# Sparse attention in one Trainium2 core: index scores, key choice and key/value products moved between the input projection's products, heads in pairs, 128 keys for the first 128 queries, token mixing in groups

## The reference

```python
xn = _rmsnorm(h, mix_norm_g[l]) * (1.0 + sc1) + sh1
proj = xn @ w_in[l]
q_a, kv_lat, q_i, k_i, w_i, p_shift, gate_a, gate_r = _split(proj, IN_SPLITS)
q = _rmsnorm(q_a by head, q_norm_g);  kv = _rmsnorm(kv_lat, kv_norm_g) @ w_kv_up
k_lin, v_lin = split(kv);  k = _rmsnorm(k_lin by head, k_norm_g)
o_attn = _dsa_attention(q, k, v, q_i, k_i, w_i)      # 8 heads of 64, 8 index heads of 32
o_rwkv = _rwkv7_time_mix(p_shift, mu, ...)
merged = sigmoid(gate_a) * (o_attn @ w_branch_attn) + sigmoid(gate_r) * (o_rwkv @ w_branch_rwkv)

# _dsa_attention, for a block of 128 queries at positions t
dots = einsum('bthd,bsd->bths', q_i, k_i)
score = einsum('bths,bth->bts', relu(dots), w_i) * idx_scale
score = where(key_pos <= t, score, -inf);   sel = top_k(score, 64)
logits = q . k[sel] / 8 - slopes[h] * (t - sel)      # slopes 2^-(h+1); masked where sel > t
o = softmax(logits) @ v[sel]

# _rwkv7_time_mix begins with
mixed = p_shift + (prev - p_shift) * mu              # prev: the token before
```

## Time and profile before

| | before |
|---|---|
| median of 3 runs | 2263.12 us (2263.04 to 2264.96) |
| the profiled execution's own time | 2260.12 us |
| its span in the trace | 2258.5 us |
| PE busy | 2089.4 us (93%) |
| DVE, ACT, POOL busy | 703.7, 277.7, 105.9 us |
| granted clock of PE, mean | 0.952 |

### The profile page before, as it was taken

How to read it: one execution, slowest core, us unless ns; L and a number is a source line. 1 busy time by engine, 2 the same in 40 slices (tenths; PEclk the granted TensorE clock), 3 DMA queues, 4 the chain that set the end, 5 groups by cost and what they waited for, 6 DMA issues and landing times.

```text
span 2258.5 us, 23974 instructions
## 1 busy us (share of the span) xinstructions
PE 2089.4 (93%) x9838; PEld 1249.5 (55%) x9838; DVE 703.7 (31%) x1237; ACT 277.7 (12%) x567; POOL 105.9 (5%) x142
## 2 busy tenths in 40 slices
PE   6999989999999999989999998586699799999998
PEld 2444444444444464457888887355588544444444
DVE  2565244424422055272433122636401400000001
ACT  2000010000000021251000011231100210000000
POOL 0010000000000020000111002000000000000000
PEclk9999999999999999999999999558899799999999
DMA  9333264424221350016774340014020699999997
GB/s 397 139 102 105 110 260 147 137 95 151 74 89 51 136 219 0 0 38 267 279 254 168 134 168 15 0 61 175 2 77 38 275 394 427 429 429 428 428 429 309
DMA packets 48186, 419.92 MB, mean 186 GB/s; under 512 B 5376, under 2 KB 5392, under 8 KB 22896
## 3 DMA queue, kind: packets, MB, share of 16 engines
q1 hardware_dynamic: 28800, 344.73, 37.5%
q0 software_dynamic: 18880, 71.18, 9.0%
q10 hardware_dynamic: 432, 2.95, 0.4%
HBM read 417.79 MB, written 1.05 MB: 185 GB/s over the span
## 4 chain that ended last, share of the span: by engine, by line
PE 81%; DVE 9%; DMA 6%; ACT 2%; issue 1%; DVEq 0%; ACTq 0%; SPq 0%; POOLq 0%
PE PS L799 17%; PE PS L816 10%; PE PS L974 8%; PE PS L1106 7%; PE PS L828 5%; DMA ring<-w_moe 4%; PE PS L962 4%; PE PS L1165 4%; PE PS L1126 4%; PE PS L1362 3%; PE PS L1139 2%; DVE SC L1443 2%; PE PS L932 2%; PE PS L773 2%; PE PS L943 2%
## 5 line engine op out<-in xcount | busy, mean ns | idle before, releaser
L799 PE MATMUL PS<-A,ring 128*128 128x512 f32 (+1 forms) x1408 | 466.3, 492 | 9.2 <-ACT A L490 9.2
L799 PEld LDWEIGHTS PS<-A,ring 128*128 128x128 f32 x1408 | 269.8, 193 | 193.9 <-issue 173.3
L816 PE MATMUL PS<-A,ring 128*128 128x512 f32 (+1 forms) x704 | 228.5, 486 | 3.2 <-DVE A L1502 3.2
L974 PE MATMUL PS<-ring,A 128*64 128x512 f32 x1024 | 223.4, 593 | 3.1 <-DMA ring<-w_moe 2.3
L816 PEld LDWEIGHTS PS<-A,ring 128*128 128x128 f32 x704 | 133.3, 190 | 96.1 <-issue 87.1
L1106 PE MATMUL PS<-A,ring 128*128 128x512 f32 x384 | 167.9, 598 | 2.0 <-ACT A L490 2.0
L974 PEld LDWEIGHTS PS<-ring,A 128*64 128x64 f32 x1024 | 73.9, 137 | 149.4 <-issue 142.7
L1443 DVE SCALAR_TENSOR_TENSOR SC<-A,CS,SC 128x512 f32<-128x512 f32 x208 | 143.7, 746 | 4.6 <-DMA A<-ada 2.2
L1106 PEld LDWEIGHTS PS<-A,ring 128*128 128x128 f32 x384 | 73.0, 192 | 91.4 <-issue 89.7
L828 PE MATMUL PS<-A,ring 128*128 128x256 f32 (+1 forms) x384 | 113.7, 458 | 9.2 <-DMA ring<-w_cout 6.8
L1502 DVE TENSOR_TENSOR A<-A,PS 128x512 f32 (+1 forms) x44 | 24.4, 554 | 304.2 <-ACT A L499 304.2
(11 more groups left out here) (308 smaller groups left out, 1976.7 us busy)
## 6 DMA issues: line engine op xcount, KB each, us to landing
ring<-w_moe SPq DMA_DIRECT2D x96, 2048.0 KB, 17.5
ring<-w_fin SPq DMA_DIRECT2D x44, 1024.0 KB, 8.1
ring<-ada POOLq DMA_DIRECT2D x64, 512.0 KB, 3.7
A<-ada POOLq DMA_DIRECT2D x64, 512.0 KB, 3.8
ring<-w_fout SPq DMA_DIRECT2D x16, 1408.0 KB, 6.1
ring<-w_conv SPq DMA_DIRECT2D x8, 1536.0 KB, 12.6
ring<-w_qkv SPq DMA_DIRECT2D x6, 2048.0 KB, 16.3
ring<-w_win SPq DMA_DIRECT2D x6, 2048.0 KB, 11.3
```

What stands on the lines that cost most here:

```text
L799: mm = pe.matmul(PS[:, 2 * (s % 3) + half, 0:T], slot(stage, s, k * 256 + half * 128, k * 256 + half * 128 + 128), h_of(k, T), start=(k == ...
L816: mm = pe.matmul(PS[:, s, 0:T], slot(stage, s, k * 128, k * 128 + 128), HID[:, k * T:(k + 1) * T], start=(k == 0), stop=(k == KF - 1))
L974: mm = pe.matmul(PS[CAP * e:CAP * (e + 1), g, :], XG[:, k * P + e * CAP:k * P + (e + 1) * CAP], slot("moe", k // 2, w, w + 512), start=(k ...
```

## The change

Five things are done, all in the third block.

*Order of the projection.* Key and value products, their head norms and the index scores are written in between the projection's products. The latent's sum of squares comes after product 4 instead of 10, `w_i` after product 8 instead of 14, head 0's dots after product 9. Banks are given explicitly.

*First block with 128 keys.* `keys(t)` is 128 for the first block of queries and 256 for the second; dots, relu, scores, key choice, attention and mixing use it.

*Key choice.* `NEGM` is made at the start of the stretch. The two blocks' MAX and MATCH_REPLACE wait for each other by counts of the semaphore `top` instead of `link`. Rounds and number of keys stay the same.

*Heads in pairs.* `dsa_attention` has the form of `na_attention`: 8 pairs, two heads in rows 0 to 63 and 64 to 127, four score banks, four buffers for probabilities. The bias matmul is gone: POOL makes the slopes times distance for all 8 heads ahead (`BIAS1`), DVE adds `SEL` once for all heads, and one DVE instruction adds the bias and takes the row maximum.

*Mixing in groups.* POOL mixes five chunks at a time, as soon as these are copied, in three groups.

```diff
+        BIAS1 = X[:, 2048:4096].rearrange("p (h t) -> p h t", h=HEADS2)
+        BIAS0 = A[:, 14848:15872].rearrange("p (h t) -> p h t", h=HEADS2)
+        def keys(t):
+            return P * (t + 1)
...
+            pool.wait_ge(sem("dist_in"), 16)
+            for h in range(HEADS2):
+                pool.tensor_scalar(BIAS1[:, h, :], DIST[:, 1, :], -(2.0 ** -(h + 1)), None, ALU.mult).then_inc(
+                    sem("bias_made"), 1)
...
-            pool.wait_ge(sem("win_copied"), len(COPIES))
             pool.wait_ge(sem("lat_done"), 2)
-            pool.tensor_tensor(d3[:, :, 1:SEQ], p3[:, :, 0:SEQ - 1], p3[:, :, 1:SEQ], ALU.subtract).then_inc(sem("mixed"), 1)
-            pool.tensor_scalar(d3[:, :, 0:1], p3[:, :, 0:1], -1.0, None, ALU.mult).then_inc(sem("mixed"), 1)
...
+            for g in range(3):
+                a, b = 5 * g, 5 * g + 5
+                pool.wait_ge(sem("win_copied"), copies_to(9 + b - 1))
+                pool.tensor_tensor(d3[:, a:b, 1:SEQ], p3[:, a:b, 0:SEQ - 1], p3[:, a:b, 1:SEQ], ALU.subtract).then_inc(
+                    sem("mixed"), 1)
...
+                pool.tensor_tensor(p3[:, a:b, :], p3[:, a:b, :], d3[:, a:b, :], ALU.add).then_inc(sem("mixed"), 2)
...
+            def dots(h):
+                r = 32 * (h % 4)
+                if h == 0:
+                    pe.wait_ge(sem("lat_root"), 1)
+                    pe.wait_ge(sem("wi_done"), 1)
+                    copied(8)
+                if h >= 2:
+                    pe.wait_ge(sem("relu"), 2 * (h - 1))
+                for t in range(2):
+                    pe.matmul(PS[:, 6 + h % 2, t * 256:t * 256 + keys(t)], QI[r:r + 32, h // 4, t * P:(t + 1) * P],
+                              KI[r:r + 32, 0:keys(t)], start=True, stop=True, tile_position=(r, 0)).then_inc(sem("dots"), 1)
...
+            for j in range(4):
+                if j < 2:
+                    copied(8 + 2 * j)
+                else:
+                    pe.wait_ge(sem("hn_done"), 20 + j - 1)
+                key_product(j, 2 * (j % 2))
+                copied(9 + 2 * j if j < 2 else 10 + j)
+                win_product(12 + j, (2 * j + 1) % 4)
+                head_stat(20 + j, 4 + j % 2)
+                dots(3 + j)
+            pe.wait_ge(sem("hn_done"), 23)
+            value_product(0, 0)
+            copied(14)
+            win_product(16, 1)
+            dots(7)
+            pe.wait_ge(sem("hn_done"), 24)
+            value_product(1, 2)
+            copied(15)
+            win_product(17, 3)
...
+            copied(23)
+            pe.wait_ge(sem("relu"), 16)
+            dsa_attention()
...
-                    pe.matmul(PS[:, u % 2, 0:256], ident, BI[:, u % 2, :], start=False, stop=True).then_inc(
-                        sem(f"s_{t}"), 1)
...
+                    for h in range(2):
+                        r = 64 * h
+                        mm = pe.matmul(PS[:, 2 * (p % 2) + h, 0:keys(t)], QA[r:r + 64, hp, t * P:(t + 1) * P],
+                                       KA[r:r + 64, hp, 0:keys(t)], start=True, stop=True)
+                    mm.then_inc(sem("s_dsa"), 1)
...
+                    link(dve.tensor_tensor_reduce(out=s, in0=s, in1=(BIAS1 if t else BIAS0)[:, h, :], scale=1.0,
+                                                  scalar=-3e38, op0=ALU.add, op1=ALU.max, accum_out=NX[:, i:i + 1]))
+                    dve.tensor_scalar(NMN[:, i:i + 1], NX[:, i:i + 1], -1.0, None, ALU.mult).then_inc(sem("max_dsa"), 1)
...
+            for t in range(2):
+                sel = SEL[:, t, 0:keys(t)]
+                link(dve.tensor_scalar(sel, SCO[:, t, 0:keys(t)], -2e38, NEG, ALU.is_gt, ALU.mult))
+                link(dve.tensor_tensor(sel, sel, NEGM[:, t, 0:keys(t)], ALU.add))
+                link(dve.tensor_tensor(BIAS1 if t else BIAS0, BIAS1 if t else BIAS1[:, :, P:2 * P],
+                                       sel.unsqueeze(1).to_broadcast([P, HEADS2, keys(t)]), ALU.add))
```

More of the change, by code:

```diff
@@ L313, in build, with copies_to @@
         COPIES = sorted(WIN)
+        def copies_to(i):
+            return sum(c <= i for c in COPIES)
         def c64(ap, c, hp, h):
@@ L1182, in _ @@
                     mm.then_inc(sem("wi_mm"), 1)
+                if i >= 9:
+                    dots(i - 9)
             slot_landed(pe, "kvup", 0)
             pe.wait_ge(sem("lat_done"), 2)
-            pe.wait_ge(sem("win_copied"), len(COPIES))
-            pe.wait_ge(sem("hn_done"), 20)
-            for i in range(4):
-                for k in range(2):
-                    mm = pe.matmul(PS[:, i, 0:SEQ], slot("kvup", 0, k * 1024 + i * 128, k * 1024 + i * 128 + 128),
-                                   LATB[:, k * SEQ:(k + 1) * SEQ], start=(k == 0), stop=(k == 1))
-                mm.then_inc(sem("hn_mm"), 1)
@@ L1203, in _ @@
-            pe.wait_ge(sem("va_copied"), 2)
-            pe.wait_ge(sem("hn_done"), 24)
-            for v in range(16):
-                t, h = divmod(v, 8)
-                r = 32 * (h % 4)
-                if v >= 4:
-                    pe.wait_ge(sem("relu"), v - 3)
-                pe.matmul(PS[:, 4 + h % 4, 0:256], QI[r:r + 32, h // 4, t * P:(t + 1) * P],
-                          KI[r:r + 32, :], start=True, stop=True, tile_position=(r, 0)).then_inc(sem("dots"), 1)
-                if v == 15:
-                    pe.wait_ge(sem("relu"), 16)
@@ L1214, in _ @@
-            attention(ATT[0])
+            for j in range(4):
+                if j < 2:
[9 more added lines that the diff above has]
+            value_product(0, 0)
@@ new lines, in _ @@
+            copied(14)
[5 more added lines that the diff above has]
+            win_product(17, 3)
+            pe.wait_ge(sem("va_copied"), 1)
+            win_product(18, 0)
+            copied(16)
+            win_product(19, 1)
+            pe.wait_ge(sem("va_copied"), 2)
+            win_product(20, 2)
+            for i in range(21, 24):
+                copied(i - 4)
+                win_product(i, (i + 2) % 4)
@@ L1550, in attention @@
-                out_copy(n // 4 - 1)
+                row_max(1)
+                for p in range(HEADS2):
+                    scale(2 * p)
+                    scale(2 * p + 1)
+                    if p + 1 < HEADS2:
+                        row_max(2 * p + 2)
+                        row_max(2 * p + 3)
+                    if p >= 2 and p % 2 == 0:
+                        out_copy(p // 2 - 1)
+                out_copy(HEADS2 // 2 - 1)
             def na_attention():
@@ L1690, in _ @@
             norm(4)
-            for i in range(4):
-                head_norm(16 + i, i)
+            dve.wait_ge(sem("dist_in"), 16)
+            link(dve.tensor_scalar(NEGM, DIST, 0.0, NEG, ALU.is_lt, ALU.mult))
+            head_norm(16, 0)
             dve.wait_ge(sem("lat_root"), 1)
@@ L1722, in _, with scored @@
-            link(dve.tensor_tensor(SEL, SEL, NEGM, ALU.add))
-            attention(ATT[0])
-            dve.wait_ge(sem("pv_dsa"), 16)
-            dve.wait_ge(sem("mixed"), 5)
+            for j in range(1, 4):
+                head_norm(16 + j, j)
+            def scored(h):
+                for t in range(2):
+                    v = 2 * h + t
+                    dve.wait_ge(sem("relu"), v + 1)
+                    if h:
+                        dve.wait_ge(sem("scored"), v - 1)
+                    sco = SCO[:, t, 0:keys(t)]
+                    dve.scalar_tensor_tensor(out=sco, in0=RL[:, v % 4, 0:keys(t)], scalar=SC3[:, t * 8 + h:t * 8 + h + 1],
+                                             in1=sco if h else NEGM[:, t, 0:keys(t)], op0=ALU.mult, op1=ALU.add).then_inc(
+                        sem("scored"), 1)
```

300 lines of the change are left out of this document (149 added, 151 removed).

## The result

The changed kernel took 2202.61 us (median of 4 runs, 2199.64 to 2205.29), the one before on the same chip 2264.04 us; the ratio is 0.9726 [0.9714, 0.9738]. The forecast was 2197 in 2184 to 2209. The profiled execution took 2203.45 us, span 2201.6.

What follows compares the result with a forecast made beforehand. Bound by 48 us of index scores and key choice, then 61.5 us of half-clock matmuls; 33.6 + 61.5 - (26.5 + 3.0) = 65.6 us gained, 2260.1 to 2194.5, plus 3.0 gives 2197; range 2184 to 2209.

Steps and rivals of the forecast that it cites:

- What bounded the kernel: Third block: 48 us of index scores and key choice ahead of everybody, then 61.5 us of small matmuls at half clock.
- Start of the attention: Projection: PE's work without a hole sums to 105.7 us, so the attention starts at 1409.2, 33.6 us gained.
- if the clock falls before 1409: Projection: a granted clock falling before the first score, near 1409, was named as a sign of being wrong.
- Nobody late: Projection: key choice, masks and bias additions stay hidden behind 26 us of PE work, 6 to 9 us to spare.
- somebody is late: Projection rival: POOL's groups delay DVE's key choice by 7 to 14 us; 2202 to 2215, 0.14 with upper PE figure.
- NEGM at nothing: Start of the projection: NEGM costs nothing there; at its old place it took 7.68 us and everybody waited.
- Attention: Attention: 26.5 us at half clock plus 3.0 for POOL's disturbance, where it took 61.5; pairs at 3.2 and 2.3.
- The fall of the clock: Attention: half clock likelier, from waits on POOL and dense work not restoring it; summed case, chance 0.50, 2192 to 2202.
- clock stays: Attention rival: full clock, 23.2 + 3.0 us, lora shortened by about 4.5; 2185 to 2191, chance 0.29.
- Pairs bring little: Attention rival: stays PE-bound at half clock near 45 us, 2213; chance 0.04 together with nothing at all.
- Everything after moves up as a block: Behind the attention: lora matmuls stay as they are and everything after moves up unchanged.
- late or upper PE: Projection or attention: somebody late, or PE pairs at 4.1 and 2.0 (3 us more); 2202 to 2215, chance 0.14.

Runs made afterwards that it cites:

- e10: Changed kernel with v's mixing behind the attention and w_i spread over products 7 and 8, plus index scores of two heads together; 2187.63 us.
- e2: Changed kernel with every mixing group waiting for all copies of the projection; 2201.30 us, attention 33.6 us.
- e8: Kernel before the change with one edit, the mask NEGM made at the start of the projection; ratio 0.9999 [0.9988, 1.0010].
- e1: Changed kernel with mixing groups of 5, 6 and 4 pieces, the last run behind the attention; attention 25.32 us.
- e9: Changed kernel with v's mixing behind the attention and w_i spread, plus filler matmuls (4, then 1, and 3 ahead of lora); attention 22.0 us.
- e4: Changed kernel with the attention by single heads, ready biases and short first block kept; attention 41.2 us.
- e7: Changed kernel with v's mixing behind the attention and w_i spread, but 256 keys for the first block too; attention ended at 25.6 us.

## Why the prediction was right, and where it was off

*What bounded the kernel* was right: both losses were real and both were removed.

*Start of the attention*: the mechanism held, the sum 105.7 was mis-sized; it measured 111.4. Row by row: product 9 in the clock's dip +1.8; the index scores 8 x 0.85 = 6.8 instead of 5.2, +1.6 (I took widths alone, and each visit to the groups of 32 rows costs something on top, e10); the first six products 23.8 instead of 22.4, +1.4, at a lower clock at their start; key products and head sums together +0.4 (the neighbours of such visits); the wait for the last copy +0.5.

The sign "if the clock falls before 1409" came in part: it fell for the length of product 9 and came back.

*Nobody late*: right, with less reserve than the 6 to 9 us stated. The last bias addition ended at 1410.5, not before 1404, 5.5 us ahead of the first score. Two errors met in that: the eight rounds of the key choice took 9.5 us (1390.4 to 1399.9) instead of 12 to 15, and the masks and bias additions behind them 10.5 instead of 5.2. In e2, where POOL is quiet at that point, the latter take 4.9, so POOL cost 5.6. The mechanism of the rival "somebody is late" was there (2.88 for 0.74, 3.25 for 1.22; the slopes kept POOL busy 6.93 us instead of 4.4), hidden by the cover.

*NEGM at nothing*: right in the changed kernel. But "everybody waited" for it was misread: e8 shows that the 7.7 us belonged to POOL's mixing, and moving NEGM alone brings nothing.

*Attention* 29.5, measured 28.5. POOL's collisions were set at 3.0 and cost 3.2 (28.5 to 25.3 in e1); the rest was set at 26.5 and took 25.3. The double pair was set at 5.5 and took 5.58. The fall of the clock was right, at 1420. One of its two reasons was not: e1 has no stall on POOL and the clock fell too. Of the rival "clock stays", e9 gives the price, with its fillers: 22.0 for the attention and 4.5 in lora, where 23.2 and 4.5 were said; but of the 4.5 only 3.2 reached the end of the `kk` stage.

*"Pairs bring little"* was rightly given little: e4 puts them at 12.7 us.

*"Everything after moves up as a block"* failed by 3 us: `kk` came 2.1 us quicker, the RWKV stage took 3.3 longer with a granted clock of 0.83 at 1500 to 1510 where before had 1.00 in the same phase, and the rest 1.8. The stage's code is the same in e8, which took 95.4 where before took 92.4; so it is the clock and not the change's work. What decides whether it dips is not settled: the fourteen profiles of that stage take either 92.1 to 92.7 or 94.6 to 95.9 us. One thing goes with it. The clock is at 0.50 when the stage begins; in the six short profiles it came back 3.0 to 3.7 us behind the stage's first matmul, in the seven that dip twice (95.4 to 95.9 us) 4.0 to 4.5 us behind it. e7, with one dip and 94.6 us, has 3.2 and does not fit. No run moved the one without the other.

Together with the late start of 1.05, these terms (+5.7, -1.0, +3.0) are 8.8 of the 9.0 us by which the profiled execution (2203.45) missed the sum (2194.5). The forecast missed the median by only 5.6, since I had added 3.0 for the distance of the profiled run from the median, and this time it lay 0.8 above it. That part of the closeness is luck. The median, 2202.61, also lies just outside the case's own range (2192 to 2202) and in that of "late or upper PE" (2202 to 2215), whose mechanisms did not occur: nobody was late, and a double pair took what was set. The case that was summed is the one that happened, a little too slow.

## What to carry to other kernels

When GpSimd and VectorE share data in SBUF, find the last GpSimd instruction before asking which VectorE instruction is slow: the wait moves to the next victim, and what removed it here was moving GpSimd's work (e1); having nothing due behind it hid it (the projection). Price small matmuls not by columns alone: a visit to the groups of 32 rows cost 0.39 us on top of its columns, and a second head in the same visit nothing. So put two heads into one visit. In a stage of short matmuls with waits, count what half clock costs downstream too; a few idle fillers that fit into the waits (four in the first, one in each later, three ahead of lora) bought 6.5 us of the stages here, and three in each wait made the attention 2.1 us longer. Do not read a stage's gain from the whole time of a few runs, when the clock elsewhere moves it by 3 us and more.

## What the runs showed of the hardware that was not expected

- A plain scaling of one SBUF tile on VectorE waited for the end of a running GpSimd addition, 2.92 us instead of 0.35. In e2 seven of sixteen were held, each until the running GpSimd instruction ended, so they are held and not slowed by a share.
- Two matmuls in two groups of 32 rows take the time of one (0.85 for four, 0.85 for two).
- Sixteen matmuls of 8 columns (3.64 us, PE busy throughout) were followed by a short stretch at 0.50 in five profiles of five (0.68 over 1345 to 1350 us in the changed kernel); spread over two products, none of it in seven of seven. Behind product 14, in one piece, they were followed by a dip in e8 and by none in the profile of before.
- Unused matmuls in PE's waits kept the clock at 1.00 through the attention in three kernels of three.
- Two profiles of one program agreed on its clock dips, but its other executions differ in mean granted clock (0.965 to 0.970) and by up to 11 us; two programs with the same stage need not agree.
